# Two of the six early expert tiles are loaded behind the reads of the first rows instead of ahead of the last scatters

## The chip, the cores and the metric

The kernel runs on one core of a Trainium2 chip. A core has five engines that run their own instruction streams and meet by semaphores: TensorE (PE in the profile; its weight loads are PEld), VectorE (DVE), ScalarE (ACT), GpSimd (POOL) and SyncE (SP), and 16 DMA engines that serve the transfers which the five issue. The metric is the device time of one execution in microseconds, lower is better.

## What is computed

The reference is a decoder trunk of two layers over 1024 tokens of width 1024, all in float32. Each layer is a mixer (attention in layer 0, a state-space part and gated DeltaNet in layer 1), a mixture of experts and a gated embedding. The change stands where a mixer ends and the experts begin:

```python
def _hier_moe(m, w_group, b_group, w_expert, b_expert, w_gate, w_up, w_down):
    ...
    experts = g_idx * MOE_PER_GROUP + e_idx      # two of 32 experts for each token
    return _expert_dispatch(xf, experts, weights, w_gate, w_up, w_down).reshape(b, s, d)

def expert_block(args):
    tok, e = args
    xb = x_pad[tok]
    hb = jax.nn.silu(xb @ w_gate[e]) * (xb @ w_up[e])
    return hb @ w_down[e]
```

Each expert has three matrices (gate, up, down) of 2 MB, so the 32 experts of a layer have 96 tiles and 201 MB of weights.

## The kernel before

The tokens are worked on in NT = 8 tiles of 128. The program is a row of stages; each is a block (`one_block`, L68), at whose end all engines meet before the next begins. Two stages matter.

**The end of the mixer** (`mixer_end`, L1153). For each of the 8 tiles of tokens TensorE makes the last projection (L1242), VectorE adds it to `h`, normalizes it to `m` and chooses two experts, and GpSimd scatters the tile's normalized rows twice (L1514), once for each chosen expert, into `c.slots_in`, a table in HBM with a region for each expert. A scatter writes 128 rows, 0.5 MB. Behind the last tile TensorE and VectorE work out the order of the experts by load; `keep_busy` (L149, L153) puts filler matmuls on TensorE between these small steps.

SyncE meanwhile issues transfers in the order of its code: residual, gain and router weights, then `own_loads`, the tiles of expert weights that are loaded early (`preloads`, L1892, EARLY = 6: gate, up and down of expert 0, then of expert 1). Tiles 0 and 1 are issued at the start, the other four once all products of the stage are done (`z["products"]` at 2 * NT). Then `clear_used` clears semaphores of the stage before. Then SyncE waits for all 16 scatters, reads the first rows of expert 0 and of expert 1 into `m` (L1221, 0.5 MB each, semaphores `c.first_in[0]` and `[1]`), and last waits until all six own tiles have landed (`z["own_in"]`). The two stages of the two layers differ only in the places of the tiles: `xt`, `place` and `s_t` in layer 0, `own`, `gdn_t`, `work`, `s_t`, `xt` and `gbz` in layer 1.

**The experts** (`first_blocks`, L1636). The experts run as units of up to 128 rows: unit 0 is expert 0, unit 1 expert 1, later ones join two experts or parts of them. For each unit TensorE turns the rows (L1728), multiplies them by gate, up and down (L1736), and turns the hidden rows between (L1748). It starts with `turn(0)`, which waits for `c.first_in[0]`; `turn(1)` comes behind the first gate product and waits for `c.first_in[1]`. The weights lie in a ring of 8 places. SyncE loads the tiles from number 6 on (L1690); tiles 6 and 7 go to free places, and each later one waits for the product that frees its place. VectorE begins the stage with the results of the routing (L1839 and on), GpSimd reads the rows of later units (L1710).

Of the kernel before, what the change touches and what calls it, by code (L numbers as in the profile page):

```python
# [18 lines left out]
NT = S // P  # L19
# [40 lines left out]
def clear_used(sp):  # L60


    while Used.sems:
        sp.sem_clear(Used.sems.pop())
# [91 lines left out]
def row(ap1d):  # L156

    return ap1d.rearrange("(a n) -> a n", a=1)
# [994 lines left out]
def mixer_end(nc, c, t, layer, h, residual, columns, slabs, slab_loads, m, mt, spare, own_loads, r, ch, delta=None, gains=None):  # L1153
# [9 lines left out]
    with ExitStack() as ctx:  # L1163
# [32 lines left out]
        with stage(nc, *names) as (block, sems):  # L1196
            z = dict(zip(names, sems))
            residual_in = [z[f"residual{n}_in"] for n in range(4)]

            @block.sync  # L1200
            def _(sp):
                with nc.allow_non_contiguous_dma(reason="router weights, short rows, column slabs"):
                    sp.dma_start(h[:, 0:2], residual.rearrange("(t p) d -> p t d", p=P)[:, 0:2]).then_inc(residual_in[0], 16)
                    for tile, view in slab_loads:
                        sp.dma_start(tile, view).then_inc(z["slabs_in"], 16)
                    for n in range(1, 4):
                        two = slice(2 * n, 2 * n + 2)
                        sp.dma_start(h[:, two], residual.rearrange("(t p) d -> p t d", p=P)[:, two]).then_inc(residual_in[n], 16)
                    sp.dma_start(gains, row(t["norm_ffn"][layer]).to_broadcast([P, D])).then_inc(z["gain_in"], 16)
                    sp.dma_start(w[:, :, 0:GROUPS], t["moe_w_group"][layer].rearrange("(k p) n -> p k n", p=P)).then_inc(z["router_in"], 16)  # L1210
                    sp.dma_start(w[:, :, GROUPS:ROUTES], t["moe_w_expert"][layer].rearrange("(k p) n -> p k n", p=P)).then_inc(z["router_in"], 16)
                    sp.dma_start(bias[:, 0:GROUPS], row(t["moe_b_group"][layer]).to_broadcast([P, GROUPS])).then_inc(z["router_in"], 16)
                    sp.dma_start(bias[:, GROUPS:ROUTES], row(t["moe_b_expert"][layer]).to_broadcast([P, EXPERTS])).then_inc(z["router_in"], 16)
                for n, (tile, view) in enumerate(own_loads):
                    if n == 2:
                        sp.wait_ge(z["products"], 2 * NT)
                    sp.dma_start(tile, view).then_inc(z["own_in"], 16)
                clear_used(sp)
                sp.wait_ge(c.scattered, (layer + 1) * 16 * 2 * NT)
                for n in range(2):  # L1220
                    sp.dma_start(m[:, n, :], c.slots_in[n * REGION:n * REGION + P, :]).then_inc(c.first_in[n], 16)  # L1221
                sp.wait_ge(z["own_in"], 16 * len(own_loads))

            @block.tensor
# [2283 lines left out]
```

## Time and profile before

| what | us |
|---|---|
| median of 3 runs | 2970.7 (2970.09 to 2974.69) |
| span of the profiled execution | 2972.4 |
| TensorE busy | 2767.0 (93%) |
| VectorE busy | 1084.5 (36%) |
| ScalarE busy | 666.5 (22%) |
| GpSimd busy | 224.4 (8%) |
| expert stage of layer 0, start of TensorE's first operation | 822.87 |
| expert stage of layer 1, the same | 2277.10 |

The span is the time from the first to the last instruction of one execution that was recorded; it stands 1.7 us over the median of the runs. Times of instructions below are counted from its start. "To landing" is the time from the start of an instruction that issues a transfer until the transfer is complete. In a timeline the bracket behind a row gives the idle time of the engine before it, and what ended that.

### The profile page before, as it was taken

The page shows a single profiled execution, that of the slowest core. Times are in us where ns is not written, and L with a number is a line of the kernel's source. Part 1 is how long each engine was busy: PE and PEld are TensorE (multiplying, and loading weights), DVE is VectorE, ACT ScalarE, POOL GpSimd, SP SyncE. Part 2 cuts the span into 40 slices and gives each one's busy share as a digit, 9 for nine tenths or more (in the row PEclk, how much of TensorE's full clock was granted, in tenths as well). Part 3 has the DMA queues.
Part 4 walks back from the last instruction along what each step waited for, and adds up shares of the span by engine and source line. Part 5 has one row for each costly group of instructions (what it writes and reads, how often), then busy time and mean ns, then how long its engine had stood idle before and what let it go on. Part 6 is the DMA issues. An engine that isn't in the chain of part 4 may idle for free. (4 is left out here: it accounts for less than half of the span.)

```text
span 2972.4 us, 41233 instructions
## 1 busy us (share of the span) xinstructions
PE 2767.0 (93%) x16685; PEld 1425.3 (48%) x16686; DVE 1084.5 (36%) x2394; ACT 666.5 (22%) x1278; POOL 224.4 (8%) x286
## 2 busy tenths in 40 slices
PE   8999999999999998899989899888998989988998
PEld 5544555555643322234467744488655323222344
DVE  3585355553510000004456635455554000000053
ACT  3310355541110000002420123333211100000132
POOL 0000000000100000002000000055211000000020
PEclk9999999999999999999999999999998999999999
DMA  4000693003499999997110120000417999999931
GB/s 167 29 29 0 251 408 134 1 37 129 183 338 407 411 412 408 405 410 276 48 47 29 17 72 29 0 3 31 159 64 287 380 410 411 406 412 404 390 127 43
DMA packets 137046, 609.38 MB, mean 205 GB/s; under 512 B 25700, under 2 KB 32260, under 8 KB 120456
## 3 DMA queue, kind: packets, MB, share of 16 engines
q1 hardware_dynamic: 113896, 529.58, 45.4%
q0 software_dynamic: 15296, 53.49, 4.9%
q10 hardware_dynamic: 7664, 23.66, 2.1%
q8 instruction: 134, 2.20, 0.3%
q14 instruction: 56, 0.46, 0.0%
HBM read 503.80 MB, written 101.71 MB: 204 GB/s over the span
## 5 line engine op out<-in xcount | busy, mean ns | idle before, releaser
L2825 PE MATMUL acc<-xt,work 128*128 128x512 f32 x384 | 166.9, 593 | 0.0
L695 PE MATMUL acc<-h,xt 128*128 128x512 f32 x384 | 165.2, 593 | 0.0
L328 PE MATMUL scores<-xt 65*128 65x512 f32 (+7 forms) x384 | 146.0, 490 | 0.4 <-DVE xt L469 0.4
L1736 PE MATMUL pg<-place 128*32 128x512 f32 (+2 forms) x736 | 137.7, 594 | 2.9 <-issue 2.9
L475 DVE TENSOR_REDUCE nmax<-scores 128x1 f32<-128x256 f32 (+7 forms) x128 | 96.8, 757 | 74.0 <-PE scores L330 71.8
L695 PEld LDWEIGHTS acc<-h,xt 128*128 128x128 f32 x384 | 73.0, 190 | 91.1 <-issue 90.8
L1242 PE MATMUL acc<-place 128*128 128x512 f32 x256 | 112.7, 595 | 1.1 <-PEq L71 1.1
L2825 PEld LDWEIGHTS acc<-xt,work 128*128 128x128 f32 x384 | 72.1, 190 | 86.0 <-issue 86.0
L1736 PE MATMUL pu<-place 128*32 128x512 f32 (+2 forms) x768 | 110.5, 617 | 0.8 <-issue 0.8
L1831 DVE COPY place<-py 128x512 f32<-128x512 f32 x21 | 14.5, 692 | 230.7 <-PE py L1736 230.7
L1831 DVE COPY work<-py 128x512 f32<-128x512 f32 x21 | 14.5, 692 | 227.7 <-PE py L1736 227.7
L422 ACT ACTIVATE s_t<-scores,nmax 128x256 f32<-128x256 f32 (+7 forms) x128 | 94.3, 737 | 8.0 <-DVE nmax L475 6.6
L1736 PE MATMUL py<-place 128*32 128x512 f32 (+2 forms) x608 | 88.2, 618 | 7.3 <-issue 7.3
L792 ACT ACTIVATE place<-acc 128x256 f32<-128x256 f32 (+4 forms) x88 | 39.8, 473 | 239.9 <-PE acc L695 239.8
L2473 PE MATMUL acc<-s_t,xt 128*128 128x260 f32 (+1 forms) x256 | 86.7, 502 | 1.1 <-PEq L71 1.1
L1864 DVE TENSOR_TENSOR work<-work,pu 128x512 f32<-128x512 f32 x21 | 14.4, 688 | 191.0 <-PE pu L1736 191.0
L1864 DVE TENSOR_TENSOR place<-place,pu 128x512 f32<-128x512 f32 x21 | 14.4, 687 | 190.3 <-PE pu L1736 190.3
L328 PEld LDWEIGHTS scores<-xt 65*128 65x128 f32 (+1 forms) x384 | 62.8, 190 | 33.1 <-issue 32.7
L1810 ACT ACTIVATE work<-pg 128x512 f32<-128x512 f32 x21 | 12.5, 597 | 289.2 <-PE pg L1736 289.2
L1810 ACT ACTIVATE place<-pg 128x512 f32<-128x512 f32 x21 | 12.5, 597 | 288.8 <-PE pg L1736 288.8
L1736 PE MATMUL pg<-own,work 128*32 128x512 f32 (+2 forms) x400 | 74.5, 600 | 2.7 <-issue 1.6
L1736 PE MATMUL pg<-xt,place 128*32 128x512 f32 (+2 forms) x400 | 74.6, 601 | 1.8 <-ACT place L1787 1.1
(758 smaller groups left out, 5416.9 us busy)
## 6 DMA issues: line engine op xcount, KB each, us to landing
place<-in_moe_w_gate_dram SPq DMA_DIRECT2D x21, 2048.0 KB, 23.6
place<-in_moe_w_up_dram SPq DMA_DIRECT2D x20, 2048.0 KB, 25.7
slots_out<-zeros SPq DMA_DIRECT2D x4, 9216.0 KB, 62.9
place<-in_moe_w_down_dram SPq DMA_DIRECT2D x18, 2048.0 KB, 26.7
xt<-in_moe_w_up_dram SPq DMA_DIRECT2D x17, 2048.0 KB, 25.2
xt<-in_moe_w_gate_dram SPq DMA_DIRECT2D x16, 2048.0 KB, 22.3
xt<-in_moe_w_down_dram SPq DMA_DIRECT2D x15, 2048.0 KB, 27.3
s_t<-in_moe_w_up_dram SPq DMA_DIRECT2D x11, 2048.0 KB, 25.3
```

Source lines behind the costliest of these rows:

```text
L328: pe.matmul(bank(n, u)[:, a * SLAB:a * SLAB + w], qkt[0:kind(p).rows, p % 2, u, 0, i * P:(i + 1) * P], qkt[0:kind(p).rows, p % 2, u, 1, a ...
L422: act.activation(probs[:, u, n % 2, 0:(i + 1) * P], bank(n, u), ACT.Exp, bias=nmax[:, n % 2, u:u + 1], accum_out=total[:, (n // NT) % 2, i ...
L475: dve.tensor_reduce(nmax[:, n % 2, u:u + 1], bank(n, u), AX.X, ALU.max, negate=True).then_inc(maxed, 1)
L695: last = pe.matmul(acc[:, n % 4, 0:width], xs[:, k, tile_of(i)], weights[:, k, cols], start=(k == 0), stop=(k == k_of - 1))
L792: last = act.activation(place, part, ACT.Copy)
L1242: last = pe.matmul(acc[:, n, :], columns(k, i), slabs[n][:, k, :], start=(k == 0), stop=(k == KD - 1))
L1736: last = pe.matmul(out[part], lhs[:, k, part], weights_of(kind, q)[:, k, cols], start=(k == 0), stop=(k == k_last), skip_group_check=True)
L1810: act.activation(gate, pg[:], ACT.Silu).then_inc(silued, 1)
L1831: dve.tensor_copy(y[:, n % 2, SLAB:D], py[:, SLAB:D]).then_inc(y_dve, 1)
L1864: dve.tensor_tensor(hid, gate, pu[:], ALU.mult).then_inc(hidden, 1)
L2473: ins = pe.matmul(acc[:, n % 4, 0:width], xt[:, k, at], slab[:, k, 0:width], start=(k == 0), stop=(k == KD - 1))
L2825: last = pe.matmul(acc[:, n % 4, :], slabs[m // 4 % 2][:, k, (m % 4) * P:(m % 4 + 1) * P], xt[:, k, half * SLAB:(half + 1) * SLAB], start= ...
```

## The change

The four own tiles behind the wait for the products become two; tile 4 is issued behind the read of the first rows of expert 0, tile 5 behind that of expert 1. The wait for all six stays where it was, as the last of the stage. The change acts in both layers.

```diff
-                for n, (tile, view) in enumerate(own_loads):
-                    if n == 2:
-                        sp.wait_ge(z["products"], 2 * NT)
-                    sp.dma_start(tile, view).then_inc(z["own_in"], 16)
+                def own(n):
+                    sp.dma_start(*own_loads[n]).then_inc(z["own_in"], 16)
+
+                own(0)
+                own(1)
+                sp.wait_ge(z["products"], 2 * NT)
+                own(2)
+                own(3)
                 clear_used(sp)
                 sp.wait_ge(c.scattered, (layer + 1) * 16 * 2 * NT)
                 for n in range(2):
                     sp.dma_start(m[:, n, :], c.slots_in[n * REGION:n * REGION + P, :]).then_inc(c.first_in[n], 16)
+                    own(4 + n)
                 sp.wait_ge(z["own_in"], 16 * len(own_loads))
```

SyncE's instructions at the end of the mixer of layer 0, before. `products`, `scattered` and `own_in` are the semaphores waited for, the barrier is the meeting of all engines, and the table is read for the expert of tile 6:

```order
L1217 DMA place<-in_moe_w_down_dram 128x4x1024 [waits products_194]
L1217 DMA place<-in_moe_w_gate_dram 128x4096
L1217 DMA place<-in_moe_w_up_dram 128x4096
L1217 DMA place<-in_moe_w_down_dram 128x4x1024
L64 ISA x23
L1221 DMA place<-slots_in 128x1024 [waits scattered]
L1221 DMA place<-slots_in 128x1024
L74 UNCONDITIONAL_BRANCH [waits own_in_187]
L1679 UNCONDITIONAL_BRANCH [waits barrier_Pool_Activation_PE_DVE_SP_release]
L1685 TENSOR_LOAD table
```

The same place in the changed kernel, whose line numbers are 4 or 5 higher behind the edit (its L1215 is L1217 of before, its L1225 is L1221):

```order
L1215 DMA place<-in_moe_w_down_dram 128x4x1024 [waits products_194]
L1215 DMA place<-in_moe_w_gate_dram 128x4096
L64 ISA x23
L1225 DMA place<-slots_in 128x1024 [waits scattered]
L1215 DMA place<-in_moe_w_up_dram 128x4096
L1225 DMA place<-slots_in 128x1024
L1215 DMA place<-in_moe_w_down_dram 128x4x1024
L74 UNCONDITIONAL_BRANCH [waits own_in_187]
L1684 UNCONDITIONAL_BRANCH [waits barrier_Pool_Activation_PE_DVE_SP_release]
L1690 TENSOR_LOAD table
```

The loads of tiles 4 and 5 have moved from ahead of the wait for the scatters to behind the first and the second read of rows; nothing else has moved, and both still stand ahead of the wait for the own tiles and of the barrier.

TensorE at the same stage switch, before and in the changed kernel; its last filler, the barrier, and the first transposes and products of the experts:

```order
L153 MATMUL o_bank<-ident 128x128 x10
L71 UNCONDITIONAL_BRANCH
L1718 UNCONDITIONAL_BRANCH [waits barrier_Pool_Activation_PE_DVE_SP_release]
L1728 MATMUL turned<-ident,place 128x128 [waits first_in0_7]
L1728 MATMUL turned<-ident,place 128x128 x7
L1736 MATMUL pg<-xt,place 128x512 [waits x_copied_235]
```

```order
L153 MATMUL o_bank<-ident 128x128 x10
L71 UNCONDITIONAL_BRANCH
L1723 UNCONDITIONAL_BRANCH [waits barrier_Pool_Activation_PE_DVE_SP_release]
L1733 MATMUL turned<-ident,place 128x128 [waits first_in0_7]
L1733 MATMUL turned<-ident,place 128x128 x7
L1741 MATMUL pg<-xt,place 128x512 [waits x_copied_235]
```

Nothing has moved on TensorE: it passes the barrier first, and then waits for the first rows.

## Rows read from the trace of the kernel before

**Rows 1.** The page's first line.

```profile
span 2972.4 us, 41233 instructions
```

**Rows 2.** Timeline of SyncE, 785 to 835: start, us, engine, line, operation, tiles, count.

```profile
789.90 0.38 SPq L1217 DMA_DIRECT2D place<-in_moe_w_down_dram  x1
790.32 0.51 SPq L1217 DMA_DIRECT2D place<-in_moe_w_gate_dram  x1
...
791.35 0.49 SPq L1217 DMA_DIRECT2D place<-in_moe_w_down_dram  x1
819.55 0.81 SPq L1221 DMA_DIRECT2D place<-slots_in  x2
821.77 0.36 SPq L1690 DMA_DIRECT2D place<-in_moe_w_gate_dram  x1
```

**Rows 3.** L1217's landings: the loads of 789.90 and 790.32; of 790.87 and 791.35.

```profile
DMA to landing us min/median/max: 8.0/10.2/12.4
...
DMA to landing us min/median/max: 17.7/22.6/27.4
```

**Rows 4.** Timeline of GpSimd, 780 to 850: the last scatter.

```profile
810.98 0.95 POOL L1514 DMA_INDIRECT slots_in<-place,slots  x1 [0.30 <-issue]
```

**Rows 5.** L1514's landings: ten scatters, 699.7 to 768.1; the pair of 783.6 and 784.9.

```profile
DMA to landing us min/median/max: 3.3/3.5/5.7
...
DMA to landing us min/median/max: 4.6/4.6/4.7
```

**Rows 6.** Timeline of VectorE and TensorE at layer 0's stage switch.

```profile
820.84 0.43 DVE L1839 TENSOR_TENSOR far<-pos,limit 128x256 f32<-128x256 f32 x1 [4.29 <-PEq L71]
...
815.50 4.62 PE L153 MATMUL o_bank<-ident 128*128 128x128 f32 x20
822.87 1.64 PE L1728 MATMUL turned<-ident,place 128*128 128x128 f32 x8 [2.75 <-DMA place<-slots_in]
825.62 9.40 PE L1736 MATMUL pg<-xt,place 128*128 128x512 f32 x16 [1.11 <-ACT place L1787]
834.85 1.06 PE L1728 MATMUL turned<-ident,place 128*128 128x128 f32 x8
835.75 7.03 PE L1736 MATMUL pu<-xt,place 128*128 128x512 f32 x16
```

**Rows 7.** The chain that ended last, at layer 1's stage switch: start, us, what.

```profile
2265.20 8.60 DMA slots_in<-work,slots
...
2273.82 3.24 DMA work<-slots_in
...
2277.10 1.78 PE turned L1728 x8
```

**Rows 8.** TensorE's waits, 890 to 1290 (total, times, longest); timeline of TensorE, 850 to 900.

```profile
PE py L1736 <- issue: 15.1, 8, 3.4
PE turned L1728 <- issue: 14.9, 7, 2.7
...
864.64 0.64 PE L1736 MATMUL pg<-s_t,place 128*64 128x512 f32 x1
```

**Rows 9.** Busy times by stretch; the last three columns: PE clock, DMA share, GB/s.

```profile
830.00:840.00 10.00, 10.00 (x30) 4.97 (x29) 0.00 (x0) 1.62 (x2) 1.02 (x2) 0.99 1.02 317
840.00:860.00 20.00, 20.00 (x57) 9.63 (x56) 2.07 (x3) 2.22 (x3) 0.53 (x1) 1.00 0.92 306
...
1000.00:1100.00 100.00, 92.72 (x804) 29.91 (x796) 8.28 (x12) 8.64 (x12) 4.00 (x8) 0.96 1.02 409
```

**Rows 10.** L1221's landings, the two reads of rows at 819.55 and 819.93.

```profile
DMA to landing us min/median/max: 3.3/3.7/4.2
```

**Rows 11.** Busy times by stretch behind the stage switch (columns as in rows 9).

```profile
828.00:830.00 2.00, 2.00 (x3) 0.67 (x2) 0.00 (x0) 0.00 (x0) 0.00 (x0) 0.50 0.99 420
...
832.00:834.00 2.00, 2.00 (x7) 0.81 (x6) 0.00 (x0) 0.00 (x0) 0.00 (x0) 1.00 0.98 287
```

**Rows 12.** Timeline of TensorE, start of the kernel.

```profile
9.50 3.69 PE L703 MATMUL turned<-ident,place 128*128 128x128 f32 x16 [9.50 <-DVE place L893]
12.99 6.15 PE L695 MATMUL acc<-place,xt 128*128 128x392 f32 x16
...
19.84 5.43 PE L695 MATMUL acc<-place,xt 128*128 128x392 f32 x16
```

## The prediction

> **What bounds the kernel now.** The page gives a span of 2972.4 us [rows 1] and a TensorE that is busy for most of it. Such a share says nothing of one place, so I read the timeline of the two places that the change touches, the end of `mixer_end` in layer 0 (about 790 to 835 us) and in layer 1 (2244 to 2289 us). They look alike: layer 0 is told, layer 1 only computed.
>
> SyncE issues the last four of the six early expert tiles in a row, from 789.90 to 791.35, and then waits for the scatters [rows 2]. The first two land 8.0 and 12.4 us after their issue, at 797.9 and 802.7, the fourth after 27.4 us, at 818.8 [rows 3]. GpSimd starts the last scatter at 810.98 [rows 4]. The ten of the earlier steps, most with little beside them, landed after 3.5 us in the median [rows 5]; this one took until SyncE's next issue at 819.55 [rows 2], 8.6 us, as layer 1's chain says outright for its own last scatter [rows 7]. So the loads hold the last scatter up by some 5 us, and SyncE's reads of the first rows follow at once.
>
> Then the stage changes. VectorE had been idle for 4.29 us when it starts the next stage's first operation at 820.84, half a microsecond after SyncE's last issue had ended (819.55 + 0.81 = 820.36); TensorE's filler ends at 820.12, and its first transposes start at 822.87, when the rows have landed [rows 6]. The reader is to see that no engine enters the expert stage before SyncE is through, and that TensorE then waits some 2 us more, for rows. From there TensorE works almost without a break until about 890. Later it waits for weights too, 15.1 and 14.9 us in the two largest groups from 890 to 1290 (the profile names "issue", but a wait for a tile of weights is what the code has there) [rows 8], while the DMA engines move 409 GB/s [rows 9].
>
> **The change, part by part.** (1) Two loads of 2 MB leave the stretch of the scatters. The two that stay should land as now, by 802.7, so the last scatter meets nothing. I take the median of the ten, 3.5 us: it lands at 814.5, 5.1 us earlier; bounds are 3.3, the least of the ten, and 4.6, the pair of 783.6 and 784.9 [rows 5]. In layer 1 it starts at 2265.20 [rows 7] and lands at 2268.7. The rule behind it is in the Trainium skill, "DMA: Bandwidth & Descriptors", section on queues, rings and completion order: each DMA engine takes turns between queues, packet by packet. The trace agrees: 8.6 us beside loads, 3.5 without.
>
> (2) The same two loads come between and behind the reads of the rows: rows 0, tile 4, rows 1, tile 5, that is 0.5, 2.1, 0.5 and 2.1 MB on SyncE's queue. The issues cost SyncE 0.3 to 0.5 us each and are covered by the transfers.
>
> (3) What stands behind them decides. SyncE's last instruction in the stage waits for all six own tiles, and the stage switch waits for SyncE. Before, it passes at once, since the fourth tile landed at 818.8. Now it is the last wait of the stage, with all engines behind it. Its length: rows 0 land 3.3 us after issue, rows 1 some 1.3 us later (4.2 us from an issue 0.38 us later) [rows 10]; a tile right behind another takes 4.8 us (802.7 less 797.9). So it is 3.3 + 4.8 + 1.3 + 4.8 = 14.2 us from the last scatter at least. On the other side a tile that starts into idle queues takes 8.0 us [rows 3]; with 0.3 us of issue and rows 0 ahead of it that makes 0.3 + 1.3 + 8.0 + 1.3 + 4.8 = 15.7. I take 14.9, the middle, as neither row is nearer. A farther bound is the stretch right behind the stage switch, where the engines were full and yet moved only 317 GB/s [rows 9]: the 4.72 MB behind rows 0 would take 14.9 us, and the whole 18.2.
>
> A check by bulk: 4.72 MB at 409 GB/s [rows 9] are 11.5 us, with the 3.3 of rows 0 14.8. The Trainium skill, "DMA: Bandwidth & Descriptors", section "Where 436 GB/s comes from", says that between HBM and SBUF a limit of about 358 GB/s per core binds. By that page the 4.72 MB would take 13.2 us and the wait 16.5, an estimate, and the kernel would end 3.2 us later than by my sum. The trace contradicts it, with 409 GB/s over 100 us, so it isn't used.
>
> (4) After the wait the switch takes 0.5 us as before. The rows have long landed, so TensorE's own wait for them goes. It starts at 814.5 + 14.9 + 0.5 = 829.9 instead of 822.87, and in layer 1 at 2268.7 + 15.4 = 2284.1 instead of 2277.10: **+7.0 us in each layer**.
>
> (5) TensorE's clock. Now it idles 2.75 us before the transposes; the new gap is 9.8 us. The clock granted from 828 to 830 is still 0.50, the lower of the two levels, 1.2 GHz, and full from 832 [rows 11]. That costs about 3.0 us now: transposes 1.64 against 1.06, the gate product 9.40 against the 7.03 of the next one [rows 6]. The nearest row for a longer gap is the start of the kernel, after 9.50 us of idleness: 3.69 us for 16 transposes against two times 1.06, and 6.15 us for the first product against 5.43 for the next [rows 12], together 2.3 us. So the longer gap should cost nothing more. Bounds are -3.0 (no slow stretch at all) and +4.7 (the whole gate product at half pace, 14.1 us against 9.40). I take 0.
>
> (6) The weight stream. Its first tile is issued at 821.77 [rows 2], 1.4 us after SyncE was through; it follows SyncE, so it moves to 829.4 + 1.4 = 830.8, by 9 us. Tile 7 is the next one behind it. With some 8 us for the first and as much for the second they land before 850; TensorE reads tile 7 first at 864.64 [rows 8], or 7 us later then. So that costs nothing. Every later tile waits for a product of TensorE that frees its place, and moves by the 7 us. The DMA engines have pockets early (306 GB/s at 92% busy from 840 to 860 [rows 9]), but TensorE's releases end them, so a late start is not caught up there. I find no slack up to the end of the stage: the 7 us go through, in both layers.
>
> Sum: 7.0 + 7.0 = +14.0 us on 2972.4, 2986.4. The profiled execution was 1.7 us over the median of the runs, 2970.7; on that scale it is 2984.7 us, 0.47% slower.
>
> **The rivals.** *A, faster: the first rows open the stage.* Were the next stage not held by the wait for the own tiles, TensorE would start once rows 0 are in (814.5 + 3.3 = 817.8) and its filler is done (820.12), near 820.2: 2.7 us earlier in each layer, 2965.3 us. For it speaks that the first products read neither tile. Against it stand the order of the instructions, with the wait for the own tiles ahead of the switch, and VectorE's idleness until SyncE was done [rows 6]. It decides where the wait lasts under 822.87 - 0.5 - 814.5 = 7.9 us: above that the change loses, and one tile alone takes 8.0. 3%.
>
> *B, the same: the delay is caught up.* If the weight stream alone set the end of the stage and its early pockets were filled (8% of 20 us, 1.6 us [rows 9]), and if the clock were up from the start (3.0 us), 7.0 a layer would shrink to 2.4: 2975.5 us. Against it: each pocket ends with a release by TensorE, and the clock was low after both gaps. 5%. That the change does nothing I exclude, since the instructions stand in the new order.
>
> *C, slower than the sum: the transfers run at the poor rate.* 18.2 instead of 14.9 us, the last scatter 4.6 instead of 3.5, and 2 of the clock's 4.7 us: 13.4 a layer, 2997.5 us. For it speaks the 317 GB/s; against it that GpSimd's reads of rows were mixed in there, while here one queue carries whole tiles. 8%.
>
> **How the numbers follow.** The sum as it stands gets 84%, A 3%, B 5%, C 8%. The low end takes 14.2 us, 3.3 for the scatter and 0.7 of the clock back (3.0 less 2.3): 7.0 - 0.7 - 0.2 - 0.7 = 5.4 a layer, 2981.5. The high end takes 18.2, 4.6 and 1 us of clock: 12.4 a layer, 2995.5. I state 2980 to 2995. A measurement of this kernel tells about 0.2%, 5.9 us, from no change. Slower by more than that: 92%; within it: 6% (B, and half of A, which lies at 5.4 us); faster: 2%.
>
> **What would show it.** Right: the last scatter lands after 3.3 to 4.6 us; tiles 4 and 5 are issued near 815 and land by 829 to 830; VectorE's idleness before the expert stage is near 13 instead of 4.29 us; TensorE's first transposes wait over 9 us, and not for rows; the weight stream's first issue moves from 821.77 to about 831; later releases come 7 us later, and the end of layer 1's expert stage 14 us later. Wrong: if TensorE starts before tile 5 has landed (A), if the shift shrinks between 830 and 1290 (B), if tile 5 lands over 16 us after the last scatter (C).

## The result and the profile after

The changed kernel takes 2988.9 us in the median of four runs (2987.72 to 2991.81). The kernel before, in the same comparison, takes 2972.69 (2970.09 to 2976.5). The ratio is 1.0058, 95% interval 1.0046 to 1.007: slower by 16.2 us in the medians, 14 to 21 us by the interval. The forecast was 14.0 us slower, 2984.7 us, range 2980 to 2995. The profiled execution of the changed kernel is the slowest of its four, so 1 to 3 us of its span say nothing of the change.

The page after begins with

```profile
span 2990.2 us, 41233 instructions
```

SyncE's timeline at the end of layer 0's mixer answers to [rows 2]. In the changed kernel L1215 issues the own tiles, L1225 the reads of rows, L1695 the weight stream:

```profile
790.23 0.38 SPq L1215 DMA_DIRECT2D place<-in_moe_w_down_dram  x1
790.65 0.51 SPq L1215 DMA_DIRECT2D place<-in_moe_w_gate_dram  x1
815.00 0.33 SPq L1225 DMA_DIRECT2D place<-slots_in  x1
815.38 0.43 SPq L1215 DMA_DIRECT2D place<-in_moe_w_up_dram  x1
815.85 0.42 SPq L1225 DMA_DIRECT2D place<-slots_in  x1
816.32 0.43 SPq L1215 DMA_DIRECT2D place<-in_moe_w_down_dram  x1
831.47 0.36 SPq L1695 DMA_DIRECT2D place<-in_moe_w_gate_dram  x1
```

The first two landings below are those of the tiles issued at 815.38 and 816.32; the third line is for the two reads of rows (3.8 and 9.2 us), which [rows 10] gave for before:

```profile
DMA to landing us min/median/max: 8.3/8.3/8.3
...
DMA to landing us min/median/max: 13.8/13.8/13.8
...
DMA to landing us min/median/max: 3.8/6.5/9.2
```

So tile 5 lands at 816.32 + 13.8 = 830.1, 15.1 us behind the first read. SyncE's own waits between 812 and 832 name it:

```profile
SPq L1225 <- DMA slots_in<-place,slots: 22.5, 1, 22.5
SPq L74 <- DMA place<-in_moe_w_down_dram: 13.3, 1, 13.3
```

Before, the first of these was 26.4 us and there was no second. GpSimd, VectorE and TensorE at the switch answer to [rows 4] and [rows 6]:

```profile
811.48 0.95 POOL L1519 DMA_INDIRECT slots_in<-place,slots  x1 [0.30 <-issue]
...
830.54 0.42 DVE L1844 TENSOR_TENSOR far<-pos,limit 128x256 f32<-128x256 f32 x1 [13.48 <-PEq L71]
...
830.54 1.94 PE L1733 MATMUL turned<-ident,place 128*128 128x128 f32 x8 [9.88 <-PEq L71]
833.60 9.18 PE L1741 MATMUL pg<-xt,place 128*128 128x512 f32 x16 [1.11 <-ACT place L1792]
842.61 1.05 PE L1733 MATMUL turned<-ident,place 128*128 128x128 f32 x8
```

The last scatter lands 3.5 us after its start (811.48 to 815.00). VectorE and TensorE enter the expert stage in the same instant, and what released TensorE is the barrier (L71), no longer the rows.

### The profile page after: what moved, and what is told of

It reads as the page before. It is cut to its first block and busy times, and to the rows that moved or that the text cites. A ratio compares the mean times of both kernels' runs of the same rounds, so it can differ in the third digit from the quotient of the medians.

```text
span 2990.2 us, 41233 instructions
## 1 busy us (share of the span) xinstructions
PE 2770.8 (93%) x16685; PEld 1427.9 (48%) x16686; DVE 1083.6 (36%) x2394; ACT 666.5 (22%) x1278; POOL 224.3 (7%) x286
## 5 line engine op out<-in xcount | busy, mean ns | idle before, releaser
L328 PEld LDWEIGHTS scores<-xt 65*128 65x128 f32 (+1 forms) x384 | 62.8, 190 | 33.1 <-issue 32.7
```

The source lines that it names most:

```text
L328: pe.matmul(bank(n, u)[:, a * SLAB:a * SLAB + w], qkt[0:kind(p).rows, p % 2, u, 0, i * P:(i + 1) * P], qkt[0:kind(p).rows, p % 2, u, 1, a ...
```

## The experiments

All times of a layer below are read from timelines in the same way. "Loads" is the issue of own tile 2 (789.90 in [rows 2]), "scatter" the start of the last scatter, "read" the first read of rows, "turn" TensorE's first transposes of the experts, "up" its first product with up weights, and "store" the first store of the embedding behind the experts. In us, layer 0 / layer 1:

| kernel | loads to scatter | scatter to read | read to turn | loads to turn | scatter to up | up to store |
|---|---|---|---|---|---|---|
| before | 21.1 / 20.9 | 8.6 / 8.6 | 3.3 / 3.3 | 33.0 / 32.8 | 24.8 / 24.8 | 579.4 / 581.4 |
| before, second profile | 22.4 / 22.4 | 7.3 / 7.4 | 3.2 / 3.3 | 32.9 / 33.1 | 23.0 / 23.3 | 579.5 / 580.9 |
| changed | 21.3 / 22.4 | 3.5 / 3.5 | 15.5 / 15.5 | 40.3 / 41.4 | 32.0 / 32.6 | 578.3 / 582.0 |
| changed, second profile | 22.4 / 21.0 | 3.5 / 3.5 | 15.6 / 15.5 | 41.5 / 40.0 | 32.4 / 31.9 | 581.7 / 577.9 |
| separate semaphores | 22.4 / 22.4 | 3.5 / 3.5 | 6.0 / 6.0 | 31.9 / 31.9 | 19.9 / 19.9 | 582.0 / 581.1 |
| the same, one tile late | 20.9 / 22.4 | 4.3 / 3.5 | 5.1 / 6.0 | 30.3 / 31.9 | 19.5 / 19.9 | 580.8 / 581.0 |
| one tile late, as changed | 22.5 / 21.0 | 3.5 / 4.1 | 11.0 / 11.0 | 36.9 / 36.1 | 27.0 / 28.2 | 584.3 / 581.3 |
| changed in layer 1 only | 22.4 / 21.1 | 7.3 / 3.5 | 3.3 / 15.6 | 33.0 / 40.2 | 23.2 / 31.9 | 587.2 / 578.2 |
| four early tiles | 21.0 / 20.9 | 3.5 / 3.5 | 5.9 / 5.9 | 30.4 / 30.3 | 19.5 / 19.5 | 588.0 / 587.0 |

**Is it the wait at the end of the stage?** The late tiles got semaphores of their own; the stage no longer waits for them, TensorE does, ahead of the product that reads each.

```diff
+    c.late_in = [ctx.enter_context(nc.semaphore(f"late_in{n}_{next(NUMBER)}")) for n in range(2)]
...
-                    own(4 + n)
-                sp.wait_ge(z["own_in"], 16 * len(own_loads))
+                    sp.dma_start(*own_loads[4 + n]).then_inc(c.late_in[n], 16)
+                sp.wait_ge(z["own_in"], 16 * 4)
...
+                    if 4 <= n < preloaded:
+                        pe.wait_ge(c.late_in[n - 4], 16 * (layer + 1))
```

> Tiles 4 and 5 are issued as in the changed kernel, but each has its own semaphore; the stage no longer waits for them, TensorE does, ahead of the first product that reads each. Theory (the wait for the own tiles at the end of the stage is the whole loss, about 10 us a layer against a stage that opens with the rows): TensorE's first transposes start near 821 instead of 830.5, as soon as its filler and the rows are through, about 2 us before the kernel before in each layer, so 2966 to 2970 us, 4 us under before. Rival (the late tiles delay the weight stream or the products themselves, and the place of the wait does not matter): within 3 us of the changed kernel's 2989.

Measured: 2971.9 us in the median, ratio to before 1.0, interval 0.9991 to 1.0009. The timelines of SyncE and TensorE, layer 0:

```profile
815.14 0.33 SPq L1226 DMA_DIRECT2D place<-slots_in  x1
815.52 0.43 SPq L1227 DMA_DIRECT2D place<-in_moe_w_up_dram  x1
816.00 0.42 SPq L1226 DMA_DIRECT2D place<-slots_in  x1
816.46 0.43 SPq L1227 DMA_DIRECT2D place<-in_moe_w_down_dram  x1
822.02 0.36 SPq L1698 DMA_DIRECT2D place<-in_moe_w_gate_dram  x1
...
821.09 1.46 PE L1736 MATMUL turned<-ident,place 128*128 128x128 f32 x8 [0.30 <-PEq L71]
823.66 7.13 PE L1744 MATMUL pg<-xt,place 128*128 128x512 f32 x16 [1.11 <-ACT place L1795]
830.63 1.05 PE L1736 MATMUL turned<-ident,place 128*128 128x128 f32 x8
```

The tiles are issued at the same times as in the changed kernel, and TensorE starts at 821.09 instead of 830.54. The whole loss of 16.2 us is gone with the wait, so the place of the wait is what made the change lose; the rival falls. The median lies 2 us over the range that was expected, because no gain is left: TensorE's first gate product ends at 830.6, against 834.9 in the first profile of before, yet the kernel is no faster.

**Half a dose in each layer.** Only tile 5 goes behind the rows, and SyncE waits for it as in the changed kernel.

```diff
                 own(3)
+                own(4)
                 clear_used(sp)
...
-                    own(4 + n)
+                own(5)
```

> Only tile 5 is loaded behind the reads of rows; tile 4 stays ahead of the last scatters, in both layers. Theory (the loss is the transfer time that stands between the last scatter and the stage switch): one tile of 4.8 to 5.5 us less in the wait, which lasts 9.5 to 10.5 us instead of 15.0, the last scatter still lands near 815; TensorE starts near 825.5, 2 to 3 us a layer after the kernel before: 2976 to 2979 us. Rival (any late tile costs a fixed amount, for the clock or the switch): over 2984 us.

Measured: 2980.16 us, ratio 1.0023, interval 1.0014 to 1.0032, so 4 to 10 us slower. From the first read to the turn it takes 11.0 us in both layers, against 15.5 with two tiles: a tile costs 4.5 us of wait. TensorE's turns lie 3 to 4 us behind those of before. The median is 1.2 us above the range that was expected, the interval reaches into it, and no fixed cost of the size of the rival (over 2984 us) shows.

**One layer alone.** The change acts only where `layer == 1`; layer 0 issues tiles 4 and 5 as before.

```diff
                 own(3)
+                if layer == 0:
+                    own(4)
+                    own(5)
                 clear_used(sp)
...
-                    own(4 + n)
+                    if layer == 1:
+                        own(4 + n)
```

> The change in layer 1 alone; layer 0 loads all six own tiles as before. Theory (each layer pays its own 7 us, and what one layer loses is not given back later): 7 to 8 us over before, 2980 to 2981 us, with layer 0 unchanged in the trace. Rival (most of the loss is in one layer): under 2977 or over 2985 us.

Measured: 2983.0 us, ratio 1.0034, interval 1.0022 to 1.0046, so 7 to 14 us. The median lies 2 us above the expected 2981, the interval holds the expected 8 as well, and the rival (under 2977 or over 2985) did not occur. Layer 0 behaves as before up to the turn (33.0 us from the loads), layer 1 as in the changed kernel (40.2). The profiled execution, the slowest of its six, needed 587.2 us from the up product to the store in layer 0, where nothing was changed and the other profiles with six early tiles show 578 to 584. So single profiles of that stretch can differ by as much as the 7 to 8 us of the effect, and a difference of that size behind the switch has to be asked of the medians.

**TensorE's clock behind the switch.** The filler ahead of the switch was made longer, first to 42, then to 53 matmuls.

```diff
-                keep_busy(pe, c, o_bank, 10)
+                keep_busy(pe, c, o_bank, 42)
```

> The changed kernel with 42 instead of 10 filler matmuls ahead of the stage switch, so that TensorE works through most of the new wait of 10 us. Theory (the longer gap costs nothing more on the clock than the short one, which costs about 3 us a layer): transposes 1.06 instead of 1.94 us, gate product 7.0 instead of 9.2 to 9.9 us, so 5 to 7 us less than the changed kernel, 2982 to 2984 us. Rival (the clock stays low behind the switch whatever ran before): unchanged, 2989 us.

Measured: 2989.37 us, ratio 1.0057, interval 1.0044 to 1.0071: unchanged. The timeline of TensorE, from 811 on and in layer 0, shows that the filler ended 2.2 us too early, and that this was enough for a slow gate product, although the last part of the filler ran at full clock. The last two lines are stretches (their last three columns as in [rows 9]):

```profile
815.70 12.26 PE L153 MATMUL o_bank<-ident 128*128 128x128 f32 x84
830.20 1.13 PE L1733 MATMUL turned<-ident,place 128*128 128x128 f32 x8 [2.24 <-PEq L71]
832.44 10.01 PE L1741 MATMUL pg<-xt,place 128*128 128x512 f32 x16 [1.11 <-ACT place L1792]
...
824.00:828.00 4.00, 3.95 (x36) 3.76 (x34) 0.00 (x0) 0.00 (x0) 0.00 (x0) 1.00 1.01 409
...
834.00:836.00 2.00, 2.00 (x3) 0.67 (x2) 1.30 (x8) 0.00 (x0) 0.55 (x1) 0.50 1.02 426
```

My theory mixed two claims, that a gap of 10 us costs no more than one of 2 to 3, and that a filler cures it. The first stands, for the second a filler up to the switch was tried:

> The changed kernel with 53 instead of 10 filler matmuls ahead of the switch, so that the filler ends at the switch and not 2 to 3 us ahead of it, as 42 did. Theory (a gap of 2 to 3 us is enough for the slow stretch behind the switch, and a gap of 10 us costs no more; with no gap it goes): transposes 1.1, gate product 7.1 us, so 2 to 3 us a layer less than the changed kernel, less up to 1 us by which the filler runs over: 2984 to 2987 us. Rival (the slow stretch comes with the switch itself): the gate product still takes over 9 us, 2989 us.

```profile
816.16 14.29 PE L153 MATMUL o_bank<-ident 128*128 128x128 f32 x106
830.75 1.13 PE L1733 MATMUL turned<-ident,place 128*128 128x128 f32 x8 [0.30 <-PEq L71]
832.99 7.13 PE L1741 MATMUL pg<-xt,place 128*128 128x512 f32 x16 [1.11 <-ACT place L1792]
```

With a gap of only 0.3 us the transposes take 1.13 and the gate product 7.13 us, against 1.94 and 9.18: 2.9 us less until the next transposes, and the rival falls. The clock needs no filler of 14 us for that: with separate semaphores, above, the 4.6 us of filler that were there before end at the switch, the gap is 0.30 us, and the gate product takes 7.13 us too.

The time hardly follows. The median is 2987.62 us, ratio 1.0056, interval 1.0042 to 1.0069, 0.6 us over the range that was expected. That is 1.3 us under the changed kernel, and by the two ratios to before (1.0056 and 1.0058) it is nothing that can be told from noise, although TensorE reaches its first product with up weights some 5 us sooner over the two layers (the filler of layer 1 ran 1.0 us over the switch, and this is taken off). So an earlier TensorE alone does not bring the time back. What was saved at the start is given back later; the section on the early opening comes back to it.

**The order of rows and tiles.** Both reads of rows stand ahead of both late tiles.

> The changed kernel with both reads of rows ahead of both late tiles. Theory (the wait is for the last byte of 5.2 MB, whatever the order): the switch is still 15.0 us behind the last scatter's landing, 2988 to 2990 us. Rival (the interleaving costs, or the second rows' read among the tiles does): 2 us or more under 2988.

Measured: 2991.0 us, ratio 1.007, interval 1.0056 to 1.0083. From the first read to the turn it takes 15.9 and 16.2 us, against 15.5, and the median is 1 us over the range that was expected. The order doesn't matter in the size that was asked; the wait is for the last byte. That it is 0.4 to 0.7 us longer is left open.

**Only the switch is late.** The kernel before, with all six tiles ahead of the last scatters, and 53 filler matmuls.

> The kernel before, all six early tiles ahead of the last scatters, with 53 instead of 10 filler matmuls, so that only the stage switch comes as late as in the changed kernel (TensorE near 830.3) and nothing else is moved. Theory (the change loses by the late switch alone): the same time as the changed kernel with the same filler, 2986 to 2989 us. Rival (a part of the loss comes from the two tiles' transfer standing later): 2 us or more under that.

Measured: 2985.59 us, ratio 1.0042, interval 1.0029 to 1.0056. TensorE's turn stood at 831.61 in layer 0, 42.1 us behind the loads in both layers. So a late switch with the early tiles left in place costs 12 us of the 16, by its interval 9 to 17. The time lies 0.4 us under the range that was expected, and under its partner with the late tiles by 2 us in the medians and 4 us by the ratios; the intervals of the two overlap, and a part of that size for the late tiles is neither shown nor excluded.

The experiment moves more than its expectation says. SyncE passes the same switch, so the weight stream is late too: its first tile is issued 43.0 us behind the loads in both layers, where it is 31.7 to 32.8 in the kernel before and 40.9 to 42.4 in the changed one. It can't tell a late TensorE from a late stream.

**What becomes of an early opening.** The first experiment opened the stage early and gained nothing. If the weight stream is the reason, the bytes that are left for it should count. Two kernels ask this: one keeps tile 4 early and gives only tile 5 its own semaphore behind the rows, the other (`EARLY = 4` in the kernel before) leaves both tiles to the weight stream.

> Tile 4 stays ahead of the last scatters; tile 5 alone goes behind the rows, has its own semaphore, and only TensorE waits for it. Theory (the weight stream sets the pace later, so bytes that are moved early count): the stage opens as early as with both tiles behind (TensorE near 821), but 2 MB less, 4.5 us of transfer, stand behind the switch in each layer, so part or all of the 2.5 us a layer that were given back there stay: 2963 to 2969 us. Rival (the bytes don't matter, the 2972 of two late tiles come from somewhere else): 2970 to 2974.

> The kernel before with four instead of six early tiles; tiles 4 and 5 are the first of the weight stream in the expert stage. Theory (the stage opens with the rows, and what is gained there is paid back where the weight stream, now two tiles longer, sets the pace): the last scatter lands near 815 and TensorE's first transposes start near 821 as with separate semaphores; tile 4 goes out some 6 us later, so 1 to 3 us above the 2972 of separate semaphores, 2971 to 2976. Rival (only the opening counts): 10 us under before, 2963.

One tile late with its own semaphore: 2965.65 us, ratio 0.998, interval 0.997 to 0.9989, **faster than the kernel before by 6 us (3 to 9) and the best of this study**; it lies in the range that was expected and outside the rival's. Four early tiles: 2980.95 us, ratio 1.0032, interval 1.002 to 1.0044, slower by 9.8 us; more than was expected by 5 us, and the rival, 2963, is far off. Yet it opens the stage as early as any:

```profile
814.42 0.80 SPq L1221 DMA_DIRECT2D place<-slots_in  x2
820.28 0.33 SPq L1690 DMA_DIRECT2D place<-in_moe_w_up_dram  x1
820.66 0.43 SPq L1690 DMA_DIRECT2D place<-in_moe_w_down_dram  x1
...
820.33 1.13 PE L1728 MATMUL turned<-ident,place 128*128 128x128 f32 x8 [0.30 <-PEq L71]
```

The stretch from 818 to 822 shows what differs from the one-tile kernel (the second line): the DMA engines have little to do until SyncE has passed the switch.

```profile
818.00:822.00 4.00, 3.16 (x18) 2.76 (x17) 1.57 (x4) 0.51 (x1) 0.00 (x0) 0.77 0.40 89
...
818.00:822.00 4.00, 2.96 (x18) 2.60 (x16) 1.74 (x5) 0.71 (x1) 0.00 (x0) 0.80 1.00 375
```

From 840 to 860 the DMA engines move 403 GB/s with two late tiles on separate semaphores and 393 with four early ones, against 306 before [rows 9]:

```profile
840.00:860.00 20.00, 20.00 (x57) 9.45 (x55) 1.38 (x2) 2.22 (x3) 1.02 (x2) 1.00 1.00 403
...
840.00:860.00 20.00, 20.00 (x59) 9.28 (x59) 1.90 (x3) 2.22 (x3) 1.02 (x2) 1.00 1.01 393
```

That is nearly the rate of the later stage (407 to 410), so little is left to fill. TensorE itself is busy for all of these 20 us, in every kernel; its waits for weights come later. From "up" to "store" the four-tile kernel takes 587 to 588 us where the others take 578 to 584, but for the 587.2 of the kernel changed in layer 1 only: the 5 us that its tiles 4 and 5 go out later (820.3 against 815.5) fit the loss, but profiles that scatter by as much don't show it.

A count over all kernels says more. The table gives what the DMA engines moved in the 110 us from the loads on, in GB/s by the views of busy times by stretch, layer 0 / layer 1 (the kernel before: 352 / 353, second profile 353 / 352). "By bytes" is an estimate: the bytes that are missing against before, in both layers, at the 409 GB/s of [rows 9]. "By TensorE" is how much later than before its first product with up weights comes, counted from the loads, both layers together. "Measured" is the median less that of the kernel before in the same comparison. All in us:

| kernel | GB/s | by bytes | by TensorE | measured |
|---|---|---|---|---|
| changed, mean of two profiles | 322 / 322 | 16.4 | 16.7 | 16.2 |
| separate semaphores | 353 / 352 | 0.0 | -6.7 | -0.3 |
| the same, one tile late | 365 / 362 | -5.9 | -8.6 | -5.5 |
| one tile late, as changed | 338 / 339 | 7.5 | 7.3 | 8.0 |
| four early tiles | 342 / 342 | 5.6 | -10.4 | 9.8 |
| changed in layer 1 only | 352 / 325 | 7.5 | 7.3 | 10.8 |
| changed, 42 fillers | 321 / 318 | 17.7 | 18.4 | 17.2 |
| changed, 53 fillers | 332 / 324 | 13.2 | 11.7 | 16.5 |
| changed, both reads first | 318 / 324 | 16.9 | 17.1 | 19.8 |
| before, 53 fillers | 325 / 324 | 15.1 | 13.1 | 11.9 |

The bytes give the sign of every loss and gain, half of the rows within 1 us, and the others within 3 to 4. TensorE's start does about as well where TensorE is late, and fails where it is early: with separate semaphores by 6 us, with one tile late by 3, with four early tiles by 20 and with the wrong sign. So the time that the DMA engines lose before the stream is under way goes with what the kernel pays, and a TensorE that starts early is held up later by the stream. This is a fit, made behind the runs: no run varies the bytes alone, the rates are of single profiles, and the 3 to 4 us of the other five rows are open.

**Second profiles.** Both kernels were profiled again to see what varies.

> The kernel before once more, for a second profile. From the last scatter of layer 0 to the first store of its embedding 604.17 us, from there to the last scatter of layer 1 850.05, from there to the first store of the output 606.19 in the first one. Theory (the middle stretch, which the change does not touch, and the weight stream differ by some us from run to run): the middle 851 to 854 us. Rival (the change itself lengthens the middle, by 2.7 us): 850.

> The changed kernel once more, for a second profile. Theory: TensorE's first transposes again 19.0 us behind the start of the last scatter in both layers (11.9 before), since that is a fixed chain; the rest of each layer's stretch 0 to 3 us off the first profile. Rival (the chain itself varies): more than 1 us off 19.0.

The middle stretch took 854.70 us in the second profile of before and 851.28 in that of after, against 850.05 and 852.77: it varies by itself, the rival falls, and the 854.70 lies 0.7 us over the range that was expected. TensorE's turn in the changed kernel stands 19.06 and 19.02 us behind the last scatter, as in the first profile: a fixed chain. From the last scatter of layer 0 to the store the second profile of the changed kernel is 3.8 us longer, in layer 1 4.9 us shorter, both beyond the 3 us that were allowed. In the kernel before, the last scatter came 22.4 us behind the loads and landed after 7.3 us, where it was 21.1 and 8.6 in the first. The gain that the forecast booked for this scatter was too large, as told below.

## Why the prediction was right, and where it was off

**(1) The last scatter.** Right in mechanism and landing: 3.5 us beside 3.5 predicted, in both layers and both profiles. The start of it was taken as given, and it is not. TensorE has filler matmuls ahead of the last ranking, and how long they take depends on how soon the granted clock rises in them. Layer 1 of the changed kernel shows it, by TensorE's timeline:

```profile
2265.55 6.13 PE L153 MATMUL o_bank<-ident 128*128 128x128 f32 x28
```

In the first profile of before the same took 4.64 us at 2257.72. Both began at a granted clock of 0.50; it was 0.90 from 2260 to 2262 in the kernel before, some 2 us into the filler, and still 0.50 from 2268 to 2270 in the changed one. So the last scatter starts 20.9 to 21.3 or 22.4 us behind the loads, by luck: what sets the moment of the rise is not shown. Before the change that costs nothing: from the loads to the read of rows it is 29.6 to 29.8 us in all four stretches of the two profiles of before. The last scatter shares the DMA engines with the loads until these are through (at 818.8 in layer 0 of the first profile), and lands within 1 us of that, whether it started early or late. With two loads gone the read follows the scatter, at 24.5 to 24.8 or 25.9 us. The 5.1 us that I booked as a gain are 4.9 to 5.3 in half of the cases and 3.6 to 3.7 in the others, 4.4 in the mean. The first profile of before had the early kind in both layers, so the rows I read could not show this; the second one had the late kind in both.

**(2), (3) The wait.** The term of 14.9 us that I took as the middle of 14.2 and 15.7 measured 15.1 (to the landing of tile 5). A tile in the queue costs 4.5 us by the kernel with one, near the 4.8 of the rows. The check by bulk, 14.8, came as near. The far bound of 18.2, by the 317 GB/s behind the switch, did not occur.

**(4) The switch.** TensorE starts in the same instant as VectorE, its wait for rows is gone, and read to turn is 15.5 us against 14.9 + 0.5 predicted. The shift of the turn was put at 7.0 us a layer. Counted from the loads it is 7.3 and 8.6 in the first profiles, 8.6 and 6.9 in the second ones, mean 7.9. Of the 0.9 us a layer beyond the sum, 0.7 are the term of (1) and 0.1 the wait.

**(5) The clock.** Taken as 0 beyond the present 3.0. Transposes and gate product together took 0.1 us more in layer 0 (1.94 + 9.18 against 1.64 + 9.40) and 0.8 us more in layer 1 of the first profiles; the mean of both profiles is 0.5 us more a layer. The bound from the start of the kernel, 0.7 us less, had the wrong sign; the value taken was near enough.

**(6) The weight stream.** The size held: from the up product to the store the mean of the two profiles is 580.0 and 579.9 us after, 579.5 and 581.2 before, so no slack takes the delay back. The stream's first tile is issued 41.7 instead of 32.3 us behind the loads in the mean of both layers and profiles, 9.4 us later, with 9 predicted. The reason that I gave, that every later tile waits for a product of TensorE and moves with it, makes TensorE's start the measure of the loss, and this failed as soon as the two were parted: TensorE is 6.7 us early over both layers with separate semaphores and gains nothing, 10.4 us early with four early tiles and loses 9.8, and 5 us earlier than in the changed kernel with 53 fillers and gains next to nothing. What the three share with their times is the bytes that the DMA engines have moved. For the change itself, TensorE's waits in layer 0 from the switch to 1330, before and after ("issue" is the wait for a tile, as in [rows 8]):

```profile
PE turned L1728 <- issue: 18.3, 8, 3.5
PE py L1736 <- issue: 15.1, 8, 3.4
PE pg L1736 <- issue: 3.5, 3, 2.4
...
PE turned L1733 <- issue: 17.3, 8, 3.3
PE py L1741 <- issue: 11.5, 8, 2.8
PE pg L1741 <- issue: 6.4, 6, 2.4
```

That is 36.9 us before and 35.2 after; layer 1 and the second profiles give 36.3 to 36.8 before and 35.1 to 36.6 after. TensorE starts 8 us later and still waits nearly as long, so the stream is as late as TensorE is. In this change the two delays have the same size, 16.7 us by TensorE's start and 16.4 by the missing bytes; that the sum of (4) could be carried through to the end was luck in that.

**The sum.** 7.9 for 7.0 us of shift gives 15.7 instead of 14.0, and the clock's 0.5 a layer 16.7: measured 16.2 in the medians. Rival A (the rows open the stage) was an error about this kernel, but its price can be judged: the kernel with separate semaphores is rival A made real. I gave it 2965.3 us; it took 2971.9. Its turn came 1.1 us a layer earlier than before, where I had 2.7, and with the clock up its first up product 3.4 us earlier; I let the early opening go through to the end, and it did not. Rival B's mechanism, the stream as the pacer, is nearer to what the runs show than the reason in (6), but not B's price: B let the stream catch up, and it did not. Rival C did not occur.

## What to carry to other kernels

When a transfer is moved behind a dependency, ask what waits for it at the end of its stage: a wait for all of a stage's loads ahead of a barrier turns a transfer that nobody needs yet into one that everybody waits for (with separate semaphores tile 4 landed at 823.9 and was first read at 853.5, tile 5 at 833.5 and 868.2). The remedy is to give it a semaphore that outlives the stage and to wait at its first reader; and even then the bytes count where a later stretch waits for the stream behind, so move as little as frees the critical transfer (here one tile of the two, 6 us gained). Count what the DMA engines have moved by a fixed point before and after, and not only when the compute engine starts. A single profile hides which of two chains that end together is the later one: read the same interval in each layer and in a second profile before a term is booked as a gain.

## What the runs showed of the hardware

- A scatter of 128 rows of 4 KB lands 3.5 us after its start where no load is in flight (3.51 or 3.52 in both layers and profiles of the changed kernel), and after 7.3 to 8.6 us beside 2 MB loads on another queue (kernel before, both profiles; 6.2 once, layer 1 of the kernel before with 53 fillers).
- TensorE's first gate product behind the stage switch was slow after every gap of over a microsecond at the switch, whatever its length; one at full clock takes 7.1 us. Gaps of 1.3 and 1.5 us (second profile of before) were followed by gate products of 8.70 and 8.73 us, one of 2.2 us behind 12 us of filler whose last part ran at full clock by 10.01 us at 0.50 (1.2 GHz), gaps of 9.8 to 9.9 us (both profiles of the changed kernel) by 9.06 to 9.85. A gap of 0.3 us gave 7.13, behind 14 us of filler and behind 4.6 us alike. With separate semaphores the clock was 0.50 from 816 to 820, during those 4.6 us, and 1.00 from 822 on; in the second profile of before it stayed at 0.50 up to 828.
- From TensorE's first up product to the first store most of a layer's 201 MB of weights are streamed. Single profiles of kernels with six early tiles took 578 to 587 us for it, so differences under some 5 us behind a change can't be read from two traces.
